# The in-projection of a hybrid attention layer as a Strassen product in two panels

## The reference

```python
shift, scale, gate = split(c @ w_ada + b_ada, 3)           # c: (1, 2048), w_ada: (2048, 6144)
h = layer_norm(x) * (1 + scale) + shift                    # (1024, 2048)
proj = h @ w_in                                            # (2048, 10760)
fq, fk, fv, flog, sq, sk, sv, g_fox, g_swa, m_fox, m_swa = split(proj)
o_fox = forgetting_attention(fq, fk, fv, cumsum(log_sigmoid(flog + b_f)))   # 8 heads of 128, causal
o_swa = sliding_window_attention(sq, sk, sv, sinks)        # 16 heads of 64, 4 kv heads, window 128, ALiBi
y = [(o * silu(g)) @ w_br for each branch]                 # (1024, 1024) @ (1024, 2048), twice
sub = (sigmoid(m_fox) * y_fox + sigmoid(m_swa) * y_swa) @ w_out
out = layer_norm(2 ** 0.25 * x + gate * sub) * ln_g + ln_b
```

## Time and profile before

| | us |
|---|---|
| median of 3 runs | 3049.2 |
| the profiled execution | 3047.21 |
| its span, first to last instruction | 3045.2 |
| PE busy | 2943.3 (97%) |
| DVE busy | 1150.8 (38%) |
| ACT busy | 862.3 (28%) |
| POOL busy | 251.1 (8%) |
| the 8112 matmuls of line 1069, mean of one | 0.39 |
| granted TensorE clock over the span | 0.985 |

### The profile page before, as it was taken

How to read it: one execution, slowest core, us unless ns; L and a number is a source line. 1 busy time by engine, 2 the same in 40 slices (tenths; PEclk the granted TensorE clock), 3 DMA queues, 4 the chain that set the end, 5 groups by cost and what they waited for, 6 DMA issues and landing times. The chain is left out here.

```text
span 3045.2 us, 37984 instructions
## 1 busy us (share of the span) xinstructions
PE 2943.3 (97%) x13561; PEld 2401.6 (79%) x13561; DVE 1150.8 (38%) x1701; ACT 862.3 (28%) x1491; POOL 251.1 (8%) x253
## 2 busy tenths in 40 slices
PE   7899999999999999999999999999988999999895
PEld 3488888888787888888888888888866888888684
DVE  6711123222113666663222222222236446644335
ACT  2511111111112444443222222222234332344111
POOL 0000000000000111110000010000012000014102
PEclk9999999999999999999999999999998999999997
DMA  9922233434223333333222222222243445556442
GB/s 311 269 69 75 69 103 107 134 107 134 63 76 82 97 90 92 93 94 90 77 71 84 76 60 88 85 78 71 83 149 124 145 163 179 169 159 193 138 141 100
DMA packets 429384, 349.23 MB, mean 115 GB/s; under 512 B 14826, under 2 KB 363034, under 8 KB 426274
## 3 DMA queue, kind: packets, MB, share of 16 engines
q1 hardware_dynamic: 387490, 281.13, 32.5%
q10 hardware_dynamic: 37538, 52.98, 4.9%
q0 software_dynamic: 4320, 14.69, 1.4%
HBM read 287.38 MB, written 61.35 MB: 115 GB/s over the span
## 5 line engine op out<-in xcount | busy, mean ns | idle before, releaser
L1069 PE MATMUL projP<-h_hi,w_hi 128*128 128x512 f32 x2704 | 1064.6, 394 | 0.0
L1069 PE MATMUL projP<-h_hi,w_lo 128*128 128x512 f32 x2704 | 1057.3, 391 | 0.0
L1069 PE MATMUL projP<-h_lo,w_hi 128*128 128x512 f32 x2704 | 1055.7, 390 | 0.0
L128 DVE TENSOR_TENSOR w_lo<-w_raw,w_hi 128x1024 fp32r<-128x1024 f32 x298 | 367.4, 1233 | 834.3 <-ACT w_hi L123 832.6
L1069 PEld LDWEIGHTS projP<-h_hi,w_lo 128*128 128x128 f32 x2704 | 508.5, 188 | 106.5
L1069 PEld LDWEIGHTS projP<-h_hi,w_hi 128*128 128x128 f32 x2704 | 508.9, 188 | 102.9 <-issue 0.9
L1069 PEld LDWEIGHTS projP<-h_lo,w_hi 128*128 128x128 f32 x2704 | 509.1, 188 | 100.8
L123 ACT CAST w_hi<-w_raw 128x1024 fp32r<-128x1024 f32 x298 | 313.9, 1054 | 844.2 <-PE projP L1069 365.8
L538 ACT COPY stage<-projP 128x512 f32<-128x512 f32 x170 | 99.7, 587 | 537.3 <-PE projP L1069 537.1
L1638 PE MATMUL yP<-og_hi,w_hi 128*128 128x512 f32 x512 | 203.5, 397 | 22.7 <-DVE og_lo L1477 20.2
L1681 PE MATMUL zP<-w_hi,mg_hi 128*128 128x512 f32 x512 | 200.4, 391 | 11.7 <-DVE w_lo L128 11.7
(11 more groups left out here) (223 smaller groups left out, 2548.3 us busy)
## 6 DMA issues: line engine op xcount, KB each, us to landing
w_raw<-in_w_in_dram SPq DMA_DIRECT2D x170, 512.0 KB, 3.8
proj_scratch<-stage ACTq DMA_DIRECT2D x170, 256.0 KB, 2.1
ada_raw<-in_w_ada_dram SPq DMA_DIRECT2D x64, 512.0 KB, 7.1
w_raw<-in_w_out_dram SPq DMA_DIRECT2D x64, 512.0 KB, 3.9
gate_raw<-in_w_ada_dram SPq DMA_DIRECT2D x16, 1024.0 KB
w_raw<-in_w_br_swa_dram SPq DMA_DIRECT2D x32, 512.0 KB, 3.9
w_raw<-in_w_br_fox_dram SPq DMA_DIRECT2D x32, 512.0 KB, 3.8
aux<-proj_scratch SPq DMA_DIRECT2D x64, 256.0 KB, 3.9
```

Source lines behind the costliest of these rows:

```text
L128: nc.vector.tensor_tensor(w_lo[:, slot, :], w_raw[:, slot, :], w_hi[:, slot, :].bitcast(F32), ALU.subtract).then_inc(chunk_lo, 1)
L1069: last = nc.tensor.matmul(projP[:, half, :], w[:, e, k * P:(k + 1) * P], hh[:, 8 * e + k, half * HALF:(half + 1) * HALF], start=(e == 0 an ...
```

## The change

**Product.** The 84 blocks become 42 groups of 256 columns. For a group, 1024 rows of the contraction (a panel) are one product of 2x2 blocks: two halves of the columns, two halves of the 1024 tokens, and even and odd slices of 128 features (4 each). A Strassen product in Winograd's form needs 7 products instead of 8, each of 4 slices x 3 parts = 12 matmuls. The seven sums and differences of h (`b_hi`, `b_lo`) are made once for a panel; those of w_in (4 of the 7, `weight_sums`) are made by POOL for each group, then all 7 are split by ACT and DVE into a ring of five slots. The first panel of all 42 groups is run first and stored; then all groups again with the second panel, whose stores add to what stands in DRAM (`accum_op=ALU.add`, issued by POOL).

```diff
+RING = (0, 1, 2, 3, 4, 1, 2)
+SUMS = {3: 0, 4: 1, 5: 2, 6: 3}
+PRE = 10
+BANKS = (pC, pA, pD, pC, pA, pC, pA)
+def product(q, k, lo=0, hi=12):
+    for n in range(lo, hi):
+        j, part = n // 3, n % 3
+        if n == 0:
+            pe.wait_ge(in_lo, 7 * q + ORDER[k])
...
+        w, b = ((ring(k, False), b_hi[:, k]), (ring(k, False), b_lo[:, LO_SLOT[k]]),
+                (ring(k, True), b_hi[:, k]))[part]
+        last = nc.tensor.matmul(BANKS[k][:], w[:, j, :], b[:, j, :], start=(k < 4 and n == 0),
+                                stop=(n == 11), skip_group_check=True)
...
+def take(q, k, n, bank, signal):
+    act.wait_ge(product_done, 7 * q + (k + 1))
...
+    nc.scalar.copy(tiles[n], bank[:]).then_inc(signal, 1)
...
+def join(q, k, n, bank, read, signal):
+    dve.wait_ge(product_done, 7 * q + (k + 1))
+    dve.wait_ge(read, q + 1)
+    nc.vector.tensor_tensor(tiles[n], bank[:], tiles[n], ALU.add).then_inc(signal, 1)
```

```diff
+def after(q, k, more=True):
+    if k == 0:
+        take(q, 0, 1, pC, t1_read)
+    if k == 1:
+        weight_high(q, 5)
+    if k == 2:
+        take(q, 2, 4, pD, t4_read)
+        weight_high(q, 6)
+        if more:
+            weight_high(q + 1, 0)
+    if k == 3:
+        take(q, 3, 2, pC, t2_read)
+    if k == 4:
+        take(q, 4, 3, pA, t3_read)
+    if k in (3, 4) and more:
+        weight_high(q + 1, k)
+    if k in (5, 6) and more:
+        weight_high(q + 1, k - 4)
```

```diff
+def load_in(q, col, panel):
...
+        sp.wait_ge(in_lo, 7 * q - 2)
+    sp.dma_start(in_raw, w_in_v[:, 8 * panel:8 * panel + 8, ds(col, 2 * P)]
+                 .rearrange("p (j e) n -> p j e n", e=2)).then_inc(in_loaded, 16)
...
+def store(q, row):
+    sp.wait_ge((n0_ready, n1_ready)[row], 2 * q + 2)
+    sp.dma_start(proj_d[ds(2 * q + row, 1), :, :].rearrange("a p t -> p (a t)"), ctile[:, row, :]
+                 ).then_inc(stored[row], 16)
...
+def group_in(q, fox, part=None):
+    if part is not None:
+        load_bg(q, part)
+    load_in(q + 1, column(q + 1, fox), 0)
+    store(q, 0)
+    store(q, 1)
```

```diff
+def weight_sums(q, which):
...
+    pool.wait_ge(in_loaded, 16 * q + 16)
+    for n in which:
+        if not first:
+            pool.wait_ge(in_lo, 7 * q + (-5, -4, -1, 0)[n])
...
+        nc.gpsimd.tensor_tensor(dst, a, b, op).then_inc(in_sums, 1)
...
+def add_group(q, row, dst):
+    pool.wait_ge((n0_ready, n1_ready)[row], 2 * q + 2)
+    pool.dma_start(proj_d[ds(dst + row, 1), :, :].rearrange("a p t -> p (a t)"), ctile[:, row, :],
+                   accum_op=ALU.add).then_inc(added[row], 16)
```

```diff
+for p in range(4):
+    ada_multiply(p)
+    if p:
+        forget(p - 1)
+    ada_turn(p)
+pe.wait_ge(ada_read, 4)
+product(0, 0, 0, 9)
+forget(3)
+product(0, 0, 9, 12)
+dense(0, 12, 84)
```

```diff
+for k in range(7):
+    after(GROUPS - 1, k)
+    if k in (0, 1):
+        renew(k)
+    if k in (5, 6):
+        renew(k - 3)
+for k in range(7):
+    after(GROUPS, k)
+    if k in (0, 1, 2):
+        renew(k + 4)
```

**Attention.** Ten groups of panel two run alone (PRE), 16 in the sliding-window units (84 matmuls each in place of 96), 16 in the heads (168 each in place of 384). The unit on PE:

```diff
+dense(q, 0, 2)
 scores(0)
+dense(q, 2, 38)
 turn_weights(0)
 scores(1)
+dense(q, 38, 48)
 weigh(0)
+dense(q, 48, 74)
 turn_weights(1)
+dense(q, 74, 84)
 weigh(1)
```

with, on DVE: maximum 0, `after(q, 1)`, reciprocal and product 0, low turned 0, maximum 1, `after` 2 and 3, output half 0, reciprocal 1, `after` 4 and 5, low turned 1, `after` 6, output half 1. ACT has the same places, `after(q, 0)` ahead of the first exponentials. POOL: product 0, `weight_sums(q + 1)`, product 1, `add_group` twice. The head, where scores of step i+1 now follow at once on the turn of step i:

```diff
+FOX_AT = (16, 22, 30, 42, 58, 78, 102, 128, 156)
+FOX_AFTER = ((), (1,), (2,), (3,), (4, 5), (6, 7), (8, 9), (10, 11, 12))
+TURNS = (0, 1, 2, 3, 4, 6, 8, 10)
...
+dense(q, 0, FOX_AT[0])
+scores(0)
+for i in range(8):
+    if i % 2 == 0 and i:
+        dense(q, FOX_AT[i], FOX_AT[i] + 8)
+        weigh(i - 1)
+        dense(q, FOX_AT[i] + 8, FOX_AT[i + 1])
+    else:
+        dense(q, FOX_AT[i], FOX_AT[i + 1])
+    turn_weights(i)
+    if i < 7:
+        scores(i + 1)
+dense(q, FOX_AT[8], 168)
+weigh(7)
```

1363 lines of the change are left out of this document (816 added, 547 removed).

## The result

The changed kernel takes 3056.9 us (median of 15 runs, 3048.7 to 3063.1) against 3048.7 us before (15 runs, 3045.6 to 3054.2): ratio 1.0024, 95% interval 1.0016 to 1.0032. Predicted were 2878. The 1104 matmuls are gone, and the time is not: it is slower by a quarter of a per cent. The profiled execution took 3048.7 us, span 3047.0, 173 us above the sum of 2875.7.

What follows compares the result with a forecast made beforehand. PE was taken to bound the kernel, busy 2943.3 of 3045.2 us. The terms sum to -171.5 from 3047.2, giving 2875.7 us profiled, 2878 as median; range for 8 in 10: 2825 to 2955.

Steps and rivals of the forecast that it cites:

- Term 1: Matmuls of the in-projection: 1104 fewer at 0.226 us each, -249.5 us.
- Term 2: Start, before the dense matmuls: halved modulation weights let dense work begin earlier, -28 us (bounds -10 to -42).
- Term 3: Plain groups of panel one: little cover for the weight load and DVE's last join, +10 us (0 to +75).
- rival A: Panel one: weights supply binds, with DVE and POOL clashing; 32 x 2.4 = 77 us, total 2945; chance 0.17.
- Term 4: Sixteen sliding-window units: PE waits 2.5 us each for POOL before the first turn, plus clock loss; +48 us (0 to +75).
- Term 5: Eight heads: fewer dense matmuls leave short PE waits, 2.2 us a head, +18 us (0 to +60).
- Steps 2 and 4 to 7 nothing: Heads: in these steps the dense matmuls before the turn cover the chain, so PE loses nothing.
- no clock term: Heads: PE's gaps are under 1 us, so no loss to a lower granted clock was counted.
- Terms 6 and 7: Other matmuls, mainly second forget-gate pass and column sums, +19 us (+12 to +22); panel change, +8 us (0 to +15).
- Term 8: Tail: output-gate loads wait for the last dense matmul, mostly hidden, +3 us (0 to +8).
- Term 9: Adding stores of panel two: land in some 7 us within the cover, 0 us (0 to very much).
- C: Attention stages run dry: units' and heads' covers at their high ends and the clock falling; total 2997; chance 0.10.

Runs made afterwards that it cites:

- third: second with earlier use of first modulation weights, 46 matmuls before a unit's first turn, k split before v, product 3 copied earlier, one tail load later: 2890.8 us.
- second: Changed kernel with five load and engine reorderings, plus earlier start sums, 42 matmuls before a unit's first turn, later pair stores in heads: 2906.6 us.

## Why the prediction was wrong

**Term 1** held: 7056 records at 0.2267.

**Term 2** (start, -28): gave nothing, +28. The x tiles take 6.2 us each, not 4.5, because DVE's statistics and scale stand in one chain with ACT's normalising; ACT copies the last one until 63.4 us, not 54. Then the transfers, which I let run through at 328 GB/s, go in four rounds of refilling and using the ring; they move 314 GB/s from 70 to 90 us and 151 to 166 from 90 to 130. Effective start was 145.3 (164.3 - 19.0), not 117; the step that failed is the end of x at 54 with an unbroken load behind it. Windows of the changed kernel, then of third, where the first round lies beside x:

```profile
50.00:70.00 20.00, 14.38 (x59) 8.03 (x57) 9.99 (x25) 12.70 (x20) 2.83 (x3) 0.75 0.00 1
70.00:90.00 20.00, 10.65 (x24) 3.10 (x23) 11.37 (x13) 5.22 (x7) 4.58 (x3) 0.66 0.97 314
```

```profile
50.00:70.00 20.00, 16.53 (x73) 8.13 (x72) 10.06 (x27) 13.37 (x22) 3.33 (x3) 0.93 0.60 196
70.00:90.00 20.00, 18.07 (x46) 4.03 (x45) 16.59 (x21) 8.64 (x11) 8.07 (x6) 0.92 0.92 299
```

In third the effective start is 139.9 - 19.0 = 120.9, four above the forecast of 117.

**Term 3** (plain groups, +10): 52, so +42. The place was right, the last join, and so was the landing (about 12, measured 11.65). The step that failed is the last join that "ends at 18.6, due 19.0": in group 9 it ended at 20.9 (354.26 - 333.34), because I had counted DVE's low parts at 0.69 in a stretch where POOL's sums stretch them, although I had named the clash and given it to rival A; it was the case. It came 25 us short of rival A's price of 77; that price itself was set too low, since 21.7 - 19.0 is 2.7 us a group, 86 us.

**Term 4** (units, +48): 63 (465.8 - 446.1 of the kernel before, and 43.4 for the matmuls that left), so +15. The wait was the one named, mis-sized: POOL was ready 12.7 to 13.1 us after the unit's start, not 12.3, and PE waited 2.6 to 3.3 us, not 2.5, which makes 7 us. The clock was named and taken too small: granted 0.97 over the 466 us, 14 us lost where 8 were forecast. It is seen in the lengths, too: the units take 28.0 and 29.9 us in turn, and from the second unit on the clock falls only in the longer ones, after waits of 2.9 to 3.3 us, and not after those of 2.6 to 2.8.

**Term 5** (heads, +18): 82, so +64, the worst. "Steps 2 and 4 to 7 nothing" failed at step 6, where PE waited 2.5 to 2.6 us, and 0.8 at step 0 was 2.0 to 3.3. Both come from loads that I took to be there: the 1 MB of weights that can't be issued before DVE's last low part of the group, and the second q block, which SP had put behind another 1 MB. The split of k cost 1.3 us a head, not 0.3 (gone in third, where k is split ahead of v), and step 3 1.3 to 1.5, not 0.6, since ACT waited for DVE's addition before its store (0.6 in second, which changes that). Together PE's waits are 59 us of the eight heads. And "no clock term" was wrong: granted 0.96 over 558 us is 22 us more. In third a head takes 63 us; forecast were 62.

**Terms 6 and 7**: 22 of term 6 lie in groups 1 to 31, as forecast. The panel change cost 14 (groups 41 and 42 took 22.9 and 29.2) instead of 8, and groups 45, 47 and 48 lost 6.5 beside DVE's operations on the forget gate (one reciprocal of 8x1024 takes 6.54 us), which the prediction did not have; with small waits elsewhere groups 32 to 51 are 14 over.

**Term 8** (tail, +3): +12 as measured, so +9. The step that failed is "the first 1 MB lands 3 us after it, where ACT's table load already stood": the table load came 16.3 us after the last dense matmul, 4.9 before, and the last store on POOL's queue, which the prediction left out here, landed 3.87 us ahead of it.

**Term 9** (adding stores, 0): the landing was right (7.1 us in the heads), and so was that ACT's waits for it cost next to nothing, though they are up to 6.2 us long; the reasoning stopped there. Beside other loads these stores cost 31 us of the heads, part of the 64 of term 5, as long as the order in the heads is the old one.

28 + 42 (term 3) + 14 (groups 32 to 51) + 15 + 64 + 9 = 172 of the 173. The rival that came truest is C (attention runs dry, with the clock), together with A: units and heads cost 145 us, where C had 185 and the forecast 66. Each rival was priced alone, and the forecast kept every cover at its best end. Of the two signs of being wrong, plain groups over 20 us came (21.4 on average in groups 1 to 31, 20.7 without term 6), a clock below 0.95 did not.

## What to carry to other kernels

When matmuls are taken out of a stage, write down for each engine the order in which it stands, with the landing of the load that each entry needs; a wait that was hidden by the slack of 12 matmuls, 2.7 us, is found there, not in the busy shares. Price DVE and POOL at their durations beside each other, and a load at its landing beside the stores that run with it. And where several delays meet at one deadline, look for the cheapest to remove: one may give back all, as the late load did here.
